# First block: GpSimd computes fifteen of each layer's sixty low parts, with a semaphore of its own

## The reference, cut to what matters

```
h = rms_norm(x, pre_norm) * (1 + scale) + shift
p = split_proj(h @ w_in)              # ret_*, dsa_*, idx_*, gla_*, merge
ret = retention(...)                  # rotated q, k; chunked decay attention
dsa = dsa_attention(...)              # 64 keys of each row picked by an index score, then softmax
gl  = gla(...)                        # gated linear attention in levels of a binary tree
y = sum over the three branches of sigmoid(merge_b) * (branch_b @ w_br_b)
x = x + gate * rms_norm(y @ w_out, post_norm)
```

## Time and profile before

| | |
|---|---|
| time, median of 3 runs | 1077.77 us (1074.63 to 1081.78) |
| the profiled execution's own time | 1075.43 us |
| its span, first to last instruction | 1073.5 us |
| TensorE busy with matmuls | 1037.6 us, 97% |
| VectorE busy | 600.8 us, 56% |
| ScalarE busy | 477.8 us, 45% |
| GpSimd busy | 76.4 us, 7% |
| mean granted TensorE clock | 0.996 |

### The profile page before, as it was taken

One profiled execution on the slowest core, in us unless ns is written; L12 is line 12 of the kernel. 1 busy time (PEld: TensorE's weight loads), 2 busy tenths in 40 slices (PEclk: granted clock), 3 DMA queues, 4 the chain that ended last, 5 costly groups with the idle time before them and its releaser, 6 DMA issues.

```text
span 1073.5 us, 13401 instructions
## 1 busy us (share of the span) xinstructions
PE 1037.6 (97%) x5148; PEld 751.6 (70%) x5148; DVE 600.8 (56%) x1177; ACT 477.8 (45%) x942; POOL 76.4 (7%) x103
## 2 busy tenths in 40 slices
PE   7999999999999999999999999999999999999997
PEld 5788875777466887757774587777677888556553
DVE  2539866595756299764455744235745555245742
ACT  3436546562144375375630353245535423225641
POOL 3001110000000021100000000500000001230000
PEclk9999999999999999999999999999999999999999
DMA  9844442477615454326467352431642016242000
GB/s 387 315 197 158 157 158 79 157 313 296 250 55 196 178 198 173 124 112 233 170 251 288 135 222 79 157 108 70 235 157 104 1 40 228 106 157 99 1 1 39
DMA packets 13742, 171.27 MB, mean 160 GB/s; under 512 B 1504, under 2 KB 1760, under 8 KB 3056
## 3 DMA queue, kind: packets, MB, share of 16 engines
q1 hardware_dynamic: 13216, 168.82, 41.2%
q10 hardware_dynamic: 464, 1.61, 0.4%
HBM read 169.37 MB, written 1.05 MB: 159 GB/s over the span
## 4 chain that ended last, share of the span: by engine, by line
PE 83%; DVE 7%; ACT 7%; DMA 2%; issue 1%; SPq 0%; DVEq 0%; ACTq 0%
PE bank L785 15%; PE bank L1123 8%; PE bank L1072 8%; PE bank L1012 7%; PE bank L1170 6%; PE bank L756 5%; PE bank L1129 5%; PE bank L1105 4%; PE bank L763 3%; PE bank L1307 3%; PE bank L857 3%; PE bank L1384 2%; PE bank L719 2%; PE bank L1372 1%; PE bank L727 1%
## 5 line engine op out<-in xcount | busy, mean ns | idle before, releaser
L1496 ACT ACTIVATE whi<-ring 128x512 fp32r<-128x512 f32 x120 | 73.8, 629 | 67.7 <-PE bank L785 67.5
L785 PE MATMUL bank<-whi,xhi 128*128 128x512 f32 (+1 forms) x256 | 99.2, 388 | 1.3 <-ACT dsag L1419 1.3
L2160 DVE TENSOR_TENSOR wlo<-ring,whi 128x512 fp32r<-128x512 f32 x120 | 82.2, 707 | 29.7 <-ACT whi L1496 29.4
L785 PE MATMUL bank<-whi,xlo 128*128 128x512 f32 (+1 forms) x256 | 97.9, 382 | 0.0
L785 PE MATMUL bank<-wlo,xhi 128*128 128x512 f32 (+1 forms) x256 | 97.4, 381 | 0.0
L763 PE MATMUL bank<-ring,hT 128*128 128x512 f32 (+1 forms) x160 | 61.8, 540 | 1.8 <-ACT hT L1439 1.8
L1129 PE MATMUL bank<-ring,hT 128*128 128x256 f32 (+2 forms) x224 | 57.9, 418 | 3.3 <-ACT hT L1462 2.3
L1012 PE MATMUL bank<-merge_high,xhi 128*128 128x512 f32 x144 | 58.5, 406 | 1.6 <-ACT retqkv L1419 1.1
L1012 PE MATMUL bank<-merge_high,xlo 128*128 128x512 f32 x144 | 57.0, 396 | 0.0
L785 PEld LDWEIGHTS bank<-whi,xhi 128*128 128x128 f32 x256 | 48.1, 188 | 12.7 <-ACT dsag L1419 1.6
L1012 PE MATMUL bank<-ring_low,xhi 128*128 128x512 f32 x144 | 56.7, 394 | 0.0
(11 more groups left out here) (412 smaller groups left out, 2182.4 us busy)
## 6 DMA issues: line engine op xcount, KB each, us to landing
ring<-in_weights SPq DMA_DIRECT2D x73, 2048.0 KB, 8.1
ring<-in_weights SPq DMA_DIRECT2D x5, 1024.0 KB, 5.1
ring<-in_weights SPq DMA_DIRECT2D x2, 1360.0 KB, 10.0
ring<-in_weights SPq DMA_DIRECT2D x1, 1536.0 KB, 8.7
kk<-in_k SPq DMA_DIRECT2D x1, 1120.0 KB, 8.1
X<-in_x SPq DMA_DIRECT2D x1, 1024.0 KB, 14.7
kc<-in_k ACTq DMA_DIRECT2D x1, 1024.0 KB, 11.9
X<-in_context SPq DMA_DIRECT2D x1, 1024.0 KB, 10.0
```

The lines of the kernel that those rows point to most:

```text
L785: mm = pe.matmul(o[:, 0:width], a, b[:, q % BUFFERS, at], start=(k == 0 and m == 0), stop=(k == KD - 1 and m == 2))
L1496: act.activation(whi1[:, q % BUFFERS, :], w, ACT.Copy).then_inc(event("hi1_ready"), 1)
L2160: dve.tensor_tensor(wlo1[:, q % BUFFERS, :], piece1(q)[2], whi1[:, q % BUFFERS, :], ALU.subtract).then_inc(event("lo1_ready"), 1)
```

## The change

GpSimd takes over the low parts of 15 of the 60 pieces of each layer. `POOL_EARLY` (5, 8, 11, 14, 17) stands ahead of the rotation of the dsa rows, `POOL_LATE` (25, 28, 31, 34, 37) behind it, and one of `POOL_LEVELS` (41, 45, 49, 53, 57) ahead of each of the first five `KL` products. GpSimd counts them on a semaphore of its own, `lo1_pooled`. VectorE skips them. TensorE waits for the one or the other semaphore ahead of each piece (`low_ready`), and SP, ahead of a refill, for the last four pieces of the old projection, one wait each. No other instruction is added or removed, and the arithmetic is the same.

```
+POOL_EARLY, POOL_LATE, POOL_LEVELS = (5, 8, 11, 14, 17), (25, 28, 31, 34, 37), (41, 45, 49, 53, 57)
+POOLED = POOL_EARLY + POOL_LATE + POOL_LEVELS
...
+        def low_ready(eng, q, l):
+
+            if q in POOLED:
+                eng.wait_ge(event("lo1_pooled"), l * len(POOLED) + sum(p <= q for p in POOLED))
+            else:
+                eng.wait_ge(event("lo1_ready"), l * (len(PIECES1) - len(POOLED)) + q + 1 - sum(p <= q for p in POOLED))
...
                         if old in SPLIT1:
-                            sp.wait_ge(event("lo1_ready"), l * len(PIECES1) + SPLIT1[old])
+                            low_ready(sp, SPLIT1[old] - 1, l)
+                            low_ready(sp, SPLIT1[old] - 2, l)
+                            low_ready(sp, SPLIT1[old] - 3, l)
+                            low_ready(sp, SPLIT1[old] - 4, l)
...
-                    pe.wait_ge(event("lo1_ready"), l * len(PIECES1) + (q + 1))
+                    low_ready(pe, q, l)
...
+                def pool_low(pieces):
+
+                    for q in pieces:
+                        pool.wait_ge(event("hi1_ready"), l * len(PIECES1) + (q + 1))
+                        pool.tensor_tensor(wlo1[:, q % BUFFERS, :], piece1(q)[2], whi1[:, q % BUFFERS, :],
+                                           ALU.subtract).then_inc(event("lo1_pooled"), 1)
+
                 for t in range(TT):
                     for h in range(2):
                         emptied(pool, u, f"xT{t}{h}")
+                pool_low(POOL_EARLY)
                 for name in ("dsa_q", "dsa_kv"):
                     for t in range(TT):
                         emptied(pool, u, f"{name}{t}")
...
                 ins.then_inc(event("dsa_rot"), 1)
 
+                pool_low(POOL_LATE)
                 emptied(pool, u, "gk")
                 for i in range(1, len(LEVELS)):
+                    pool_low(POOL_LEVELS[i - 1:i])
                     pool.wait_ge(event("gexp"), l * 8 + i)
...
                 def low(first, last):
 
                     for q in range(first, last):
+                        if q in POOLED:
+                            continue
                         dve.wait_ge(event("hi1_ready"), l * len(PIECES1) + (q + 1))
```

## The result

The changed kernel takes 1080.34 us, median of 20 runs (1077.86 to 1083.31), beside 1077.35 us for the kernel before in the same runs. The ratio is 1.0026, with a 95% interval of 1.0016 to 1.0037: a loss of about 2.8 us, between 1.7 and 4.0. 1082.6 was predicted, from a median of 1077.77 for the kernel before and a loss of 4.8 us. The profiled execution took 1078.94 us, its span 1077.0.

What follows compares the result with a forecast made beforehand. TensorE, busy 97% of the span, was taken as the bound; 0.5 + 1.8 + 2.5 = 4.8 us on 1075.4 gives 1080.2, and the median's 2.3 more gives 1082.6 us; loss 2 to 7 us, range 1079.5 to 1085.

Steps and rivals of the forecast that it cites:

- The most it can gain: TensorE's only listed wait for VectorE is the retention rotation; gain costed at 0, bounded by 0.8 us.
- The price of a pooled piece: One low part on GpSimd takes 1.29 us; the new wait itself costs TensorE nothing below about 3.0 us an instruction.
- the starved rival: GpSimd's instruction is much dearer because it writes fp32r; loss passes 10.8 us at 2.7 us an instruction; chance 0.09.
- Piece 4: Layer 0: GpSimd's piece 5 holds the port, so VectorE's low part 4 ends 0.4 to 0.6 us late; taken as 0.5.
- The dsa rotation and low part 24: Each layer: GpSimd's later dsa rotation, or low part 24 held by piece 25; 0.9 us a layer, twice 1.8 us.
- the alternative: If the dsa rotation is not late, VectorE reaches low part 24 late, behind GpSimd's piece 25; 1.1 us late.
- The retention rotation: Each layer: GpSimd's piece 37 goes ahead of line 2236's fourth product, delaying TensorE by 1.25 us, twice 2.5 us.
- The 0.74 us of the earlier trace as a ceiling: Longest collision wait seen before the change; using it would make the retention rotation term 1.5 us and the sum 3.8.
- The gla levels: `KL` of the first five levels comes 1.3 us later, or 3 to 4, hidden by four pieces between; costed at 0.

Runs made afterwards that it cites:

- the two repeats of the kernel after: The changed kernel, unaltered, traced twice more; openings 46.28 and 46.38 us, layer 0 26.50 and 26.51 us, layer 1 25.59 and 25.60 us.
- no25_37: The changed kernel with pieces 25 and 37 given back to VectorE, 13 a layer left on GpSimd; ratio 1.0009 to the kernel before.
- half37: The changed kernel with GpSimd doing 256 of piece 37's 512 columns and VectorE the other 256; ratio 1.0022 to the kernel before.
- early19: The changed kernel with piece 19 also given to GpSimd, ahead of the dsa rotation; ratio 1.013 to the kernel before.

## Why the prediction was right, point by point

The mechanism was right: turns at SBUF between the two engines, at places where TensorE waits. The size was too large: the 4.8 us of the sum lie above the measured interval of 1.7 to 4.0, and it is the wide range of 2 to 7 us that holds the 2.8.

- **The most it can gain: right.** Nothing came back anywhere. Low part 35 waited 1.12 us for its high part in place of the 0.52 of the earlier trace rows, as said: VectorE came earlier and waited longer. That `ret_rot` was the one wait for VectorE was too narrow a reading: the view lists 3.1 us for the scaled rows of line 2087 (2109 after) too, the same before and after.
- **The price of a pooled piece: right.** 1.29 us with its fp32r output, as for the f32 product of the earlier trace rows; the mean of 1369 ns has GpSimd's own turns of waiting in it. TensorE never waited for a pooled low part, so the starved rival is out. (By its own formula, that rival passes 10.8 us at 2.8 us an instruction and not at 2.7.)
- **Piece 4, 0.5 us in layer 0: right in most executions, a little small.** 0.5 to 0.9 us in the eight traces with five early pieces in which the opening ran at its usual pace, absent in the one with a dip of the clock just before. What held VectorE was one of the two 80-column instructions that end the index rotation; the prediction had low part 4 itself held.
- **The dsa rotation and low part 24, 0.9 us a layer: right in its parts, over-sized in the sum.** This is the term that was mis-sized. The rotation is not late, with 0.54 us to spare where 0.75 was worked out. What I gave as the alternative happened: VectorE, 0.6 us late against TensorE (95.77 - 89.67 in place of 93.35 - 87.85), asks for low part 24 in the same 0.04 us in which GpSimd asks for 25. Taken at 1.8 us for both layers, it was 0 in one execution of the changed kernel and 0.9 in each of the other two. That the order could fall either way I did not see: the 0.9 that I took is what a lost turn costs, and it is lost in some layers only.
- **The retention rotation, 2.5 us: right, 2.2 measured.** 1.10 us a layer, to 0.02 us in every kernel that has it. The full turn is 1.29 us; VectorE's fourth product grew by 1.09. The prediction read from the earlier trace rows that a held instruction ends one free duration behind the other's end; in that row it is 120.04 - 119.50 = 0.54 us and not 0.69, and so it is here, which is most of the difference. The 0.74 us of the earlier trace rows as a ceiling, with a sum of 3.8, was the worse choice for this term. The Trainium skill, "SBUF — State Buffer", section "SBUF: two separate sides", has the loser of the port blocked for the whole instruction; by the 1.09 of 1.29 us this trace agrees.
- **The gla levels, 0: right.** From the retention transposes of one layer to the dsa transposes of the next the two repeats of the kernel after need 274.79 and 276.49 us, the kernel before 274.78. The first has one dip of the clock there, as the kernel before has, and the second one more.

Averaged over the three traced executions of the changed kernel, piece 4 makes 0.5 us (0, 0.7 and 0.8), low part 24 0.6 (0, 0.9 and 0.9) and the retention rotation 2.2: 3.3 us, where 4.8 was predicted and 2.8 (1.7 to 4.0) measured. What is left of the difference lies within the interval.

## What to carry to other kernels

Moving the subtraction of two SBUF tiles from VectorE to GpSimd did not take it out of VectorE's way: each piece moved could hold VectorE for most of a GpSimd instruction (1.1 of 1.29 us, where VectorE would have spent 0.69), and it got in between two VectorE instructions that stand back to back. So before moving a piece, look at what VectorE runs in the microsecond after its input is ready; if that chain ends in something the bounding engine waits for, leave it. And read first what the chain waits for: here one low part moved by two places on VectorE took away the wait that fifteen pieces moved to another engine made longer.

## What the runs showed of the hardware that I had not expected

- **A tie is decided by hundredths of a microsecond.** GpSimd was recorded ahead of VectorE in all sixteen layers: by 13 to 34 ns where VectorE went first, by 36 to 43 ns where GpSimd did. The kernel after showed both. It is worth 0.9 us a layer here.
- **A held instruction ends 0.14 us short of a free duration behind the other's end.** A VectorE instruction of 512 columns (0.69 us free) ended 0.54 to 0.56 us behind GpSimd's end in the retention rotation, at low part 24, at low part 27 of no25_37 and in half37. The 80-column one of the first repeat, with 0.23 us in the kernel before, took 1.35 and ended 0.10 behind. It holds the other way too: GpSimd's piece 25, held in the trace after, ended at 97.59, 1.14 us behind VectorE's end at 96.45, with 1.29 free. So what is lost depends on how far the other one is when an instruction asks, and hardly on its own length.
- **Waits of 3 us cost more than their length.** During the two waits of early19 (3.0 us for TensorE's matmuls, 3.4 for its weight loads) the granted clock fell to its lower level; the rows of 10 us above have means of 0.66 and 0.83, and the stretches that followed were 2.7 and 1.3 us longer. At the waits of 1.5 us for the retention rotation none of the traces of the changed kernel shows a fall. The length of a single wait is not the whole of it: in the kernel before the clock fell at about 235.8 us, 2 us behind a wait of 1.34. What decides those falls in the opening and between the layers, which kernels before and after have alike, stays open.
